# Top-k rounds, masks and evacuations reordered in the mixing stage of a two-block transformer kernel

## The chip, the cores and the metric

The kernel runs on one core of one Trainium2 chip, as one program. Time is device microseconds (us) of one execution. The core's engines are TensorE (PE, its weight loads PEld), VectorE (DVE), ScalarE (ACT), GpSimd (POOL) and SyncE (SP); each runs its own instructions in order, and they wait for each other by semaphores that only count up. Matrix products go into PSUM (8 banks of 128 partitions by 512 float32), everything else lies in SBUF.

## The reference, cut to what matters

Two transformer blocks on 512 tokens of width 1024, all in float32. The change lies in the mixing stage of the second block:

```
z = u @ w_in          # split into aq, ak, av, iq, ik, iw, rq, rk, rv, rg, ga, gb
...
score = sum over 8 index heads of relu(q_idx . k_idx) * w_idx      # per query and key
score = where(admissible, score, -1e30)                            # chunks of 64
top_val, top_pos = top_k(score, 128)
y_a = softmax attention of 8 heads over the selected keys
rq, rk = rope(rq), rope(rk)                     # 4 heads of 128
y_r = group_norm(retention(rq, rk, rv)) * silu(rg)
merged = sigmoid(ga) * (y_a @ w_branch_a) + sigmoid(gb) * (y_r @ w_branch_b)
```

## The kernel before, in words

All products are made in three passes of rounded parts: an operand x is held as a high part and a low part (XH, XL; HH, HL), a weight as WH and WL, and PE adds high*high, low*high and high*low. Weights come in units of 128 x 1024 (512 KB) in one fixed order. SP fetches a unit into one of 4 slots of RAW; POOL rounds it (L326, WH = RAW * 1) and takes the rest (L329, WL = RAW - WH); PE uses it and counts `units_done`, which frees the slot for POOL and SP. Unit n of a feature-major product goes to PSUM bank n mod 4, and DVE counts `evacuated` (started at 4, as are the other unit counts) when a bank has been read. Unit numbers are held in FIRST: the mixing stage has mix_heads from 252, ret_qk from 263, ret_v from 271, ret_gate from 279, merge from 287.

The order around the change, all written out by hand:

- *Index scores.* PE makes the scores of tile t (128 queries against 128(t+1) keys) of 8 heads, ACT takes the relu, DVE adds them up in SC (L1551, L1554). DVE then writes -1e30 where a key may not be seen (L1561) and copies tiles 1 to 3 to MK (L1563). Tile 0 has 128 keys, so all are taken.
- *Top-k.* `take(first, rounds)` does rounds of `max` (the 8 largest of each query, to TOP, L1571) and `match_replace` (those set to -3e38 in MK, L1572). Sixteen rounds give the 128 keys of a tile: rounds 0 to 15 are tile 1 (256 columns), 16 to 31 tile 2 (384), 32 to 47 tile 3 (512).
- *Rotations.* The eight units of ret_qk are rotated by `rotate`: it waits for the unit, does what `between` holds (two rounds of take), waits for ACT's copy with swapped halves (L1077, into bank 7), multiplies by cosine (L1527, which frees the bank), by sine (L1528), adds (L1529).
- *Value halves.* `products_token_major` makes retention's values for 512 of 1024 channels at a time: 4 units, 96 matmuls (L437), into all four banks 0 to 3, one per 128 tokens. PE waits for a bank when it first writes to it, at k = 0. DVE evacuates a half with four instructions (`token_major`, L1448, from PSUM to VT). `order` is the order of the four.
- *Masks.* For each tile DVE makes an additive mask, 0 or -1e30, in MK from SC and MK (L1583 to L1587), from SBUF to SBUF: two `tensor_scalar` for tile 0, three and one `tensor_tensor` for each other tile.
- *Sparse attention.* 16 steps s = 4p + t (head pair p, tile t). PE: scores(s) into banks 4 and 5 (L755), transposes(s-1) (L765), two k steps of the gate products (ret_gate, L371 to L373, banks 2 and 3), values(s-1) into bank 0 or 1 (L776). DVE: adds the mask and takes the maximum (L1608), two reciprocals, one scaling (L1620). ACT: exponentials, the other scaling, copies. scores(s) waits until both heads of s-1 are masked (`a_masked`).

In the kernel before, PE waits ahead of all of this for all four evacuations of the second value half, and the first two gate units wait for them again.

Of the kernel before, what the change touches and what calls it, by code (L numbers as in the profile page):

```python
# [31 lines left out]
TT = SEQ // P  # L32
SLOTS = 4
# [32 lines left out]
FIRST = {name: sum(n for _, n in PRODUCTS[:k]) for k, (name, _) in enumerate(PRODUCTS)}  # L66
# [51 lines left out]
def program(nc, xT, weights, gains, cols, lnb, bs, wsT, rel, pos, ident_d, decay, pT, out):  # L118
    with ExitStack() as ctx:
# [73 lines left out]
        def sem(name):  # L193
            return ctx.enter_context(nc.semaphore(name))
# [6 lines left out]
        evacuated = sem("evacuated")  # L201
# [64 lines left out]
        def n_of(t):  # L266

            return P * (t + 1)

        def off(t):  # L270

            return P * (t * (t + 1) // 2)
# [68 lines left out]
        def _(pe):  # L341
# [28 lines left out]
            def three_passes(bank_, slot, w, xh, xl, k, stop):  # L370
                nc.tensor.matmul(PS[:, bank_, :], WH[:, slot, w], xh[:, k, :], start=(k == 0), stop=False)  # L371
                nc.tensor.matmul(PS[:, bank_, :], WH[:, slot, w], xl[:, k, :], start=False, stop=False)  # L372
                return nc.tensor.matmul(PS[:, bank_, :], WL[:, slot, w], xh[:, k, :], start=False, stop=stop)  # L373

            def together(*units, norm=True):
# [5 lines left out]
                for k in range(tiles):  # L381
                    w = slice(k * P, k * P + P)
                    for s, (_, xh, xl, ready) in enumerate(units):
                        slot = (first + s) % SLOTS
                        if k == 0:
                            pe.wait_ge(weights_split, split.next())
                            pe.wait_ge(evacuated, bank.next())
                            high.next()
                        if ready is xr:
                            if s == 0:  # L390
                                pe.wait_ge(xh_ready, xg.now(back=tiles - 1 - k))
                            if k == tiles - 1 and s >= 2:
                                continue
                            high_passes(slot, w, xh, k)
                    if norm and k == tiles - 1:
                        stat_sum()
                    for s, (_, xh, xl, ready) in enumerate(units):
                        slot = (first + s) % SLOTS
                        if s == 0:
                            pe.wait_ge(ready.sem, ready.now(back=tiles - 1 - k))  # L400
                        if ready is not xr:
                            last = three_passes(slot, slot, w, xh, xl, k, k == tiles - 1)
                        else:
                            if k == tiles - 1 and s >= 2:
                                high_passes(slot, w, xh, k)
                            last = low_pass(slot, w, xl, k, tiles)
                        if k == tiles - 1:
                            last.then_inc(units_done, 1)
                        if norm and k == tiles - 1 and s == 2:
                            stat_spread()  # L410
# [321 lines left out]
            products_token_major()  # L732

            g0 = FIRST["ret_gate"]
            pe.wait_ge(evacuated, g0 + SLOTS)
            pe.wait_ge(rotated, 18)

            def gate_products(first, last):

                for j in range(first, last):  # L740
                    n, k = g0 + j // DT, j % DT
                    if k == 0:
                        pe.wait_ge(weights_split, n + 1 + SLOTS)
                        pe.wait_ge(evacuated, n + 3)
                    end = three_passes(2 + n % 2, n % SLOTS, slice(k * P, k * P + P), XH, XL, k, k == DT - 1)
                    if k == DT - 1:
                        end.then_inc(units_done, 1)
# [21 lines left out]
            def sparse_values(s):  # L769
                p, t = divmod(s, TT)  # L770
                pe.wait_ge(a_turned_out, 2 * s + 2)
                if t == 0 and p >= 2:
                    pe.wait_ge(a_low, p - 1)
                for k in range(t + 1):
                    for hh in range(2):
                        last = nc.tensor.matmul(PS[hh * HD:hh * HD + HD, p % 2, t * P:t * P + P], AVW[:, k, 0:HD],  # L776
                                                PROBT[:, hh, k * P:k * P + P], start=(k == 0), stop=(k == t))
                        if k == t:
                            last.then_inc(a_values, 1)
# [28 lines left out]
            for s in range(steps):  # L808
                sparse_scores(s)
                if s:  # L810
                    sparse_transposes(s - 1)
                gate_products(2 * s, 2 * s + 2)
                if s:
                    sparse_values(s - 1)
            gate_products(32, 34)
            sparse_transposes(steps - 1)
            pe.wait_ge(a_masked, 2 * steps)
            for k in (1, 3, 0):
                ret_scores(0, k)
            sparse_values(steps - 1)  # L820
            ret_scores(0, 2)
            gate_products(34, 38)
            pe.wait_ge(a_low, 4)
            for h in range(4):
# [366 lines left out]
        def _(dve):  # L1191
            dve.sem_inc(evacuated, SLOTS)
            V = nc.vector
            done = Count(units_done, SLOTS)
# [5 lines left out]
            def link(ins):  # L1200

                ins.then_inc(dve_self, 1)
                dve.wait_ge(dve_self, me.next())
# [240 lines left out]
            def token_major(half, order=range(TT)):  # L1444
                first = done.n
                dve.wait_ge(units_done, done.next(4))
                for j in order:
                    V.tensor_scalar(VT[:, j, half * SEQ:half * SEQ + SEQ], PS[:, (first + j) % SLOTS, :],  # L1448
                                    RT[:, 4 + j:5 + j], None, ALU.mult).then_inc(evacuated, 1)
# [27 lines left out]
            for s in range(DT * TT):  # L1477
                p, t = divmod(s, TT)
                n = n_of(t)
# [41 lines left out]
            def rotate(dst, cos, sin, scale, between=None):  # L1521

                src = unit()
                if between:
                    between()
                dve.wait_ge(act_out, ao.next())
                V.scalar_tensor_tensor(T[:, 2, :], src, scale, cos, ALU.mult, ALU.mult).then_inc(evacuated, 1)  # L1527
                link(V.scalar_tensor_tensor(SWAP, SWAP, scale, sin, ALU.mult, ALU.mult))  # L1528
                V.tensor_tensor(dst, T[:, 2, :], SWAP, ALU.add).then_inc(rotated, 1)  # L1529
# [14 lines left out]
            for n in range(32):  # L1544
                t, h = n // 8, n % 8
                s = SC[:, off(t):off(t) + n_of(t)]
# [12 lines left out]
            for t in range(TT):  # L1559
                s = SC[:, off(t):off(t) + n_of(t)]  # L1560
# [4 lines left out]
            def take(first, rounds):  # L1565


                for r in range(first, first + rounds):
                    t = 1 + r // 16
                    work = MK[:, off(t):off(t) + n_of(t)]  # L1570
                    link(V.max(TOP[:], work))  # L1571
                    link(V.match_replace(work, TOP[:], work, TAKEN))  # L1572

            for n in range(8):
                rotate(R1[:, n, :], COS128, SIN128, 1.0 if n % 2 == 0 else P ** -0.5,
                       lambda: take(2 * n, 2))
            for half in range(2):
                take(16 * (half + 1), 16)
                token_major(half)
            for t in range(TT):  # L1580
                c = slice(off(t), off(t) + n_of(t))
                ok = SC[:, c]
                link(V.tensor_scalar(ok, ok, 0.5 * NEG, None, ALU.is_gt))  # L1583
                if t:
                    link(V.tensor_scalar(MK[:, c], MK[:, c], 0.5 * TAKEN, None, ALU.is_lt))
                    link(V.tensor_tensor(ok, ok, MK[:, c], ALU.mult))
                link(V.tensor_scalar(MK[:, c], ok, -NEG, NEG, ALU.mult, ALU.add))  # L1587

            def take_gate(f):

                dve.wait_ge(units_done, FIRST["ret_gate"] + f + 1 + SLOTS)
                V.tensor_tensor(gate_tile(f), PS[:, 2 + (FIRST["ret_gate"] + f) % 2, :], RI[:], ALU.mult)\
                 .then_inc(evacuated, 1)
# [6 lines left out]
            for s in range(4 * TT):  # L1600
                p, t = divmod(s, TT)
                n = n_of(t)
# [249 lines left out]
```

## Time and profile before

| | us |
|---|---|
| median of 3 runs | 2481.31 (2479.49 to 2481.4) |
| the profiled execution | 2479.67 |
| its span in the profile | 2477.9 |
| PE busy | 2399.2 (97%) |
| DVE busy | 1112.5 (45%) |
| ACT busy | 563.3 (23%) |
| POOL busy | 1739.4 (70%) |

Times in the rows further below are microseconds from the span's start. In a timeline a row is: start, duration, engine, line and operation, output<-inputs with partitions x elements, the number of like instructions merged in it (xN), and in brackets the idle time of the engine ahead of it with the engine and instruction that ended it. No bracket means that the engine was idle for next to nothing. An instruction's duration holds what it waits for after it was issued, a busy port for instance.

### The profile page before, as it was taken

The page shows a single profiled execution, that of the slowest core. Times are in us where ns is not written, and L with a number is a line of the kernel's source. Part 1 is how long each engine was busy: PE and PEld are TensorE (multiplying, and loading weights), DVE is VectorE, ACT ScalarE, POOL GpSimd, SP SyncE. Part 2 cuts the span into 40 slices and gives each one's busy share as a digit, 9 for nine tenths or more (in the row PEclk, how much of TensorE's full clock was granted, in tenths as well). Part 3 has the DMA queues.
Part 4 walks back from the last instruction along what each step waited for, and adds up shares of the span by engine and source line. Part 5 has one row for each costly group of instructions (what it writes and reads, how often), then busy time and mean ns, then how long its engine had stood idle before and what let it go on. Part 6 is the DMA issues. An engine that isn't in the chain of part 4 may idle for free.

```text
span 2477.9 us, 31448 instructions
## 1 busy us (share of the span) xinstructions
PE 2399.2 (97%) x11070; PEld 1941.6 (78%) x11070; DVE 1112.5 (45%) x1584; ACT 563.3 (23%) x1039; POOL 1739.4 (70%) x827
## 2 busy tenths in 40 slices
PE   8999999999999999999999999998999999999998
PEld 6777888877777788887888888676678888888876
DVE  3445323454444532447424335478573334342345
ACT  2322101132553210113201013321621121010031
POOL 8657877776445787785888887565248887888765
PEclk9999999999999999999999999999999999999999
DMA  5222333323222233332233323232112333333322
GB/s 180 85 68 85 102 93 100 95 85 100 84 68 69 77 102 95 94 104 77 86 109 93 100 85 100 64 102 68 31 51 89 102 102 94 94 96 99 89 73 77
DMA packets 64665, 221.08 MB, mean 89 GB/s; under 512 B 7360, under 2 KB 9664, under 8 KB 64448
## 3 DMA queue, kind: packets, MB, share of 16 engines
q1 hardware_dynamic: 60336, 210.27, 28.4%
q10 hardware_dynamic: 4240, 9.57, 1.3%
q8 instruction: 62, 1.02, 0.2%
q14 instruction: 27, 0.22, 0.0%
HBM read 217.71 MB, written 2.10 MB: 89 GB/s over the span
## 4 chain that ended last, share of the span: by engine, by line
PE 89%; DVE 6%; ACT 2%; issue 2%; DMA 0%; DVEq 0%; POOL 0%; ACTq 0%; SPq 0%; POOLq 0%
PE PS L366 21%; PE PS L360 21%; PE PS L361 21%; PE PS L437 4%; PE PS L371 4%; PE PS L373 4%; PE PS L372 4%; PE PS L413 1%; PE PS L414 1%; PE PS L417 1%; PE PS L637 1%; DVE MK L1572 1%; PE PS L658 1%; PE PS L647 1%; DVE TOP L1571 1%
## 5 line engine op out<-in xcount | busy, mean ns | idle before, releaser
L326 POOL TENSOR_TENSOR WH<-RAW,ONES 128x1024 fp32r<-128x1024 f32 (+3 forms) x411 | 767.1, 1866 | 682.0 <-PE PS L366 270.8
L329 POOL TENSOR_TENSOR WL<-RAW,WH 128x1024 fp32r<-128x1024 f32 (+3 forms) x411 | 976.8, 2377 | 32.2
L360 PE MATMUL PS<-XH,WH 128*128 128x512 f32 x1568 | 615.9, 393 | 9.8 <-DVE PTL L1698 5.4
L361 PE MATMUL PS<-XL,WH 128*128 128x512 f32 x1568 | 613.2, 391 | 0.0
L366 PE MATMUL PS<-XH,WL 128*128 128x512 f32 x1568 | 387.9, 389 | 0.0
L360 PEld LDWEIGHTS PS<-XH,WH 128*128 128x128 f32 x1568 | 296.4, 189 | 80.1 <-issue 10.9
L361 PEld LDWEIGHTS PS<-XL,WH 128*128 128x128 f32 x1568 | 296.3, 189 | 61.0
L366 PEld LDWEIGHTS PS<-XH,WL 128*128 128x128 f32 x1568 | 294.0, 188 | 62.8 <-issue 1.6
L1312 DVE TENSOR_TENSOR HL<-T,HH 128x512 f32 x108 | 233.5, 2162 | 152.1 <-ACT HH L945 107.7
L360 PE MATMUL PS<-HH,WH 128*128 128x512 f32 x712 | 277.2, 389 | 2.0 <-DVE HL L1632 2.0
L361 PE MATMUL PS<-HL,WH 128*128 128x512 f32 x712 | 277.0, 389 | 0.0
L1342 DVE TENSOR_TENSOR M<-PS,M 128x512 f32 x80 | 55.2, 692 | 312.8 <-PE PS L366 278.1
L366 PE MATMUL PS<-HH,WL 128*128 128x512 f32 x712 | 177.1, 390 | 0.0
L360 PEld LDWEIGHTS PS<-HH,WH 128*128 128x128 f32 x712 | 133.6, 188 | 30.5 <-DVE HL L1632 2.7
L366 PEld LDWEIGHTS PS<-HH,WL 128*128 128x128 f32 x712 | 134.0, 188 | 27.9
L361 PEld LDWEIGHTS PS<-HL,WH 128*128 128x128 f32 x712 | 133.6, 188 | 27.7
L942 ACT ACTIVATE T<-T 128x512 f32<-128x512 f32 x64 | 40.6, 635 | 485.0 <-DVE T L1319 485.0
L1329 DVE TENSOR_TENSOR T<-PS,RI 128x512 f32<-128x512 f32 x44 | 30.4, 691 | 193.1 <-PE PS L366 193.1
L371 PE MATMUL PS<-HH,WH 128*128 128x512 f32 x280 | 110.7, 395 | 5.7 <-POOL WL L329 5.4
L373 PE MATMUL PS<-HH,WL 128*128 128x512 f32 x280 | 109.2, 390 | 0.0
L372 PE MATMUL PS<-HL,WH 128*128 128x512 f32 x280 | 109.0, 389 | 0.0
L957 ACT ACTIVATE HH<-T 128x512 f32 x44 | 27.9, 634 | 279.8 <-DVE T L1332 279.8
(232 smaller groups left out, 2941.4 us busy)
## 6 DMA issues: line engine op xcount, KB each, us to landing
RAW<-in_weights SPq DMA_DIRECT2D x379, 512.0 KB, 3.5
RAW<-in_weights SPq DMA_DIRECT2D x16, 384.0 KB, 3.1
H<-in_xT SPq DMA_DIRECT2D x8, 256.0 KB, 6.4
BIAS<-in_rel ACTq DMA_DIRECT2D x8, 256.0 KB, 3.4
RAW<-in_weights SPq DMA_DIRECT2D x8, 256.0 KB, 2.7
out<-R ACTq DMA_DIRECT2D x8, 256.0 KB, 2.2
BIAS<-in_rel ACTq DMA_DIRECT2D x8, 224.0 KB, 3.8
DECAY<-in_decay ACTq DMA_DIRECT2D x1, 1024.0 KB, 4.7
```

Source lines behind the costliest of these rows:

```text
L326: nc.gpsimd.tensor_tensor(WH[:, slot, 0:w], raw, ONES[:, 0:1].to_broadcast([P, w]), ALU.mult).then_inc(high_split, 1)
L329: nc.gpsimd.tensor_tensor(WL[:, slot, 0:w], raw, WH[:, slot, 0:w].bitcast(F32), ALU.subtract).then_inc(weights_split, 1)
L360: nc.tensor.matmul(PS[:, slot, :], WH[:, slot, w], xh[:, k, :], start=(k == 0), stop=False)
L361: nc.tensor.matmul(PS[:, slot, :], WH[:, slot, w], xl[:, k, :], start=False, stop=False)
L366: last = nc.tensor.matmul(PS[:, slot, :], WL[:, slot, k * P:k * P + P], xh[:, k, :], start=False, stop=(k == tiles - 1))
L371: nc.tensor.matmul(PS[:, bank_, :], WH[:, slot, w], xh[:, k, :], start=(k == 0), stop=False)
L372: nc.tensor.matmul(PS[:, bank_, :], WH[:, slot, w], xl[:, k, :], start=False, stop=False)
L373: return nc.tensor.matmul(PS[:, bank_, :], WL[:, slot, w], xh[:, k, :], start=False, stop=stop)
L437: return nc.tensor.matmul(PS[:, (first + j) % SLOTS, :], x[:, k, j * P:j * P + P], wt[:, slot, kk * SEQ:kk * SEQ + SEQ], start=(k == 0 and ...
L942: S.activation(T[:, 1, :], T[:, 0, :], ACT.Square).then_inc(act_self, 1)
L1312: V.tensor_tensor(HL[:, f, :], T[:, src:src + 1, :], HH[:, f, :].bitcast(F32), ALU.subtract).then_inc(h_ready, 1)
L1342: V.tensor_tensor(M[:, f, :], PS[:, slot:slot + 1, :], M[:, f, :], ALU.add)\
```

## The change

- DVE does three rounds beside each rotation instead of two (24 instead of 16), then 8 rounds.
- The masks of tiles 0 to 2 are made after these, then come 4 rounds of tile 3, then the evacuation of the first value half, then the other 12 rounds.
- The second value half is evacuated with the two gate banks (3 and 2) first, then 0 and 1; the mask of tile 3 follows.
- PE no longer waits for the four evacuations ahead of the attention: the first gate unit waits for one of them, the second for two, and values(0), the first to write to bank 0, for all four.

```diff
             g0 = FIRST["ret_gate"]
-            pe.wait_ge(evacuated, g0 + SLOTS)
             pe.wait_ge(rotated, 18)
...
                     if k == 0:
                         pe.wait_ge(weights_split, n + 1 + SLOTS)
-                        pe.wait_ge(evacuated, n + 3)
+                        pe.wait_ge(evacuated, n + 3 if n >= g0 + 2 else n + 1)
...
             def sparse_values(s):
                 p, t = divmod(s, TT)
                 pe.wait_ge(a_turned_out, 2 * s + 2)
+                if s == 0:
+                    pe.wait_ge(evacuated, g0 + SLOTS)
...
             for n in range(8):
                 rotate(R1[:, n, :], COS128, SIN128, 1.0 if n % 2 == 0 else P ** -0.5,
-                       lambda: take(2 * n, 2))
-            for half in range(2):
-                take(16 * (half + 1), 16)
-                token_major(half)
-            for t in range(TT):
+                       lambda: take(3 * n, 3))
+            def mask(t):
+
                 c = slice(off(t), off(t) + n_of(t))
                 ok = SC[:, c]
                 link(V.tensor_scalar(ok, ok, 0.5 * NEG, None, ALU.is_gt))
...
                 link(V.tensor_scalar(MK[:, c], ok, -NEG, NEG, ALU.mult, ALU.add))
+            take(24, 8)
+            for t in range(3):
+                mask(t)
+            take(32, 4)
+            token_major(0)
+            take(36, 12)
+            g0 = FIRST["ret_gate"]
+            banks = (2 + g0 % 2, 2 + (g0 + 1) % 2, 0, 1)
+            token_major(1, [(b - done.n) % SLOTS for b in banks])
+            mask(3)
```

## Rows read from the trace of the kernel before

**Rows 1.** The page, part 1: busy us (share of the span) xinstructions.

```profile
PE 2399.2 (97%) x11070; PEld 1941.6 (78%) x11070; DVE 1112.5 (45%) x1584; ACT 563.3 (23%) x1039; POOL 1739.4 (70%) x827
```

**Rows 2.** Timeline of PE: start, us, what, [idle before it <-releaser].

```profile
1666.49 0.50 PE L437 MATMUL PS<-WH,XH 128*128 128x512 f32 x1 [0.71 <-DVE T L1527]
...
1688.50 0.50 PE L437 MATMUL PS<-WH,XH 128*128 128x512 f32 x1 [2.00 <-DVE VT L1448]
...
1717.40 0.80 PE L755 MATMUL PS<-AK,AQIQ 64*128 64x128 f32 x4 [6.79 <-DVE VT L1448]
...
1723.68 0.70 PE L755 MATMUL PS<-AK,AQIQ 64*128 64x256 f32 x4 [2.62 <-DVE NMX L1608]
```

**Rows 3.** Timeline of DVE, rotations of ret_qk and the rounds behind.

```profile
1627.95 0.43 DVE L1571 MAX8 TOP<-MK 128x8 f32<-128x256 f32 x1
...
1629.92 0.69 DVE L1527 SCALAR_TENSOR_TENSOR T<-PS,ROT 128x512 f32<-128x512 f32 x1
...
1658.34 0.43 DVE L1571 MAX8 TOP<-MK 128x8 f32<-128x256 f32 x1 [1.45 <-PE PS L366]
...
1665.74 0.69 DVE L1527 SCALAR_TENSOR_TENSOR T<-PS,ROT 128x512 f32<-128x512 f32 x1
...
1667.68 0.56 DVE L1571 MAX8 TOP<-MK 128x8 f32<-128x384 f32 x1
```

**Rows 4.** Timeline of DVE, evacuations, last rounds, masks, first step of the attention.

```profile
1687.69 2.73 DVE L1448 TENSOR_SCALAR VT<-PS,RT 128x512 f32<-128x512 f32 x4
1690.34 0.68 DVE L1571 MAX8 TOP<-MK 128x8 f32<-128x512 f32 x1
...
1714.62 2.73 DVE L1448 TENSOR_SCALAR VT<-PS,RT 128x512 f32<-128x512 f32 x4
1717.26 0.22 DVE L1583 TENSOR_SCALAR SC<-SC 128x128 f32<-128x128 f32 x1
...
1721.00 0.43 DVE L1583 TENSOR_SCALAR SC<-SC 128x512 f32<-128x512 f32 x1
...
1723.11 0.29 DVE L1608 CUSTOM_DVE_ANT_0 PROB<-PS,MK 128x128 f32<-128x128 f32 x1
```

**Rows 5.** Timeline of POOL, the splits of weight units.

```profile
1675.71 1.90 POOL L326 TENSOR_TENSOR WH<-RAW,ONES 128x1024 fp32r<-128x1024 f32 x1 [1.05 <-PE PS L437]
1677.68 2.40 POOL L329 TENSOR_TENSOR WL<-RAW,WH 128x1024 fp32r<-128x1024 f32 x1
1681.15 1.90 POOL L326 TENSOR_TENSOR WH<-RAW,ONES 128x1024 fp32r<-128x1024 f32 x1 [1.06 <-PE PS L437]
...
1712.66 2.35 POOL L329 TENSOR_TENSOR WL<-RAW,WH 128x1024 fp32r<-128x1024 f32 x1
1735.25 1.90 POOL L326 TENSOR_TENSOR WH<-RAW,ONES 128x1024 fp32r<-128x1024 f32 x1 [20.24 <-PE PS L373]
...
1849.93 2.69 POOL L329 TENSOR_TENSOR WL<-RAW,WH 128x1024 fp32r<-128x1024 f32 x1
```

**Rows 6.** Timeline of DVE, two instructions that meet POOL at work.

```profile
1735.99 1.43 DVE L1620 TENSOR_SCALAR PROB<-PROB,RECX 128x512 f32<-128x512 f32 x1
...
1850.32 2.84 DVE L1632 SCALAR_TENSOR_TENSOR HL<-R,GAIN,HH 128x512 fp32r<-128x512 f32 x1
```

**Rows 7.** The page, part 5: a group of instructions | busy us, mean ns | idle before.

```profile
L1312 DVE TENSOR_TENSOR HL<-T,HH 128x512 f32 x108 | 233.5, 2162 | 152.1 <-ACT HH L945 107.7
```

**Rows 8.** Windows: us, busy PE, PEld, DVE, ACT, POOL, then PEclk, DMA share, GB/s.

```profile
1689.00:1692.00 3.00, 3.00 (x14) 2.37 (x14) 2.93 (x7) 0.00 (x0) 1.96 (x1) 1.00 0.00 0
...
1714.50:1715.00 0.50, 0.00 (x0) 0.00 (x0) 0.47 (x2) 0.00 (x0) 0.50 (x1) 0.78 0.00 0
...
1717.00:1720.00 3.00, 2.60 (x8) 1.99 (x9) 2.74 (x9) 0.00 (x0) 0.00 (x0) 0.50 0.28 113
...
1721.50:1722.00 0.50, 0.00 (x0) 0.00 (x0) 0.47 (x2) 0.00 (x0) 0.00 (x0) 0.89 0.00 0
1726.00:1729.00 3.00, 3.00 (x13) 1.56 (x11) 0.68 (x3) 1.01 (x5) 0.00 (x0) 0.59 0.00 0
```

## The prediction

> **What bounds the kernel now.** I read the page's busy line first: TensorE (PE) is busy for 97% of the span [rows 1]. So a change matters only where PE stands still, and the mixing stage has the one long place: 6.79 us for VectorE (DVE) at 1710.6 us, then 2.62 us more at 1721 [rows 2]. Next, DVE's timeline: it shows why PE waits. From 1667.68 on DVE has no gap in brackets: sixteen rounds of 384 columns, four evacuations, sixteen rounds of 512 columns, four evacuations, the masks, and at 1723.11 the first L1608 of the sparse attention [rows 3, 4]. DVE is the bound there, though in the rotations before it it stood idle, mostly 1.45 us each time [rows 3]. L1608 is the point of account: PE's second scores follow 0.57 us behind it [rows 2, 4], then PE is nearly gapless, so what L1608 gains or loses the end does too. Last, GpSimd's (POOL) timeline beside DVE's, since the change moves work in time: POOL stands idle for 20.24 us from 1715.0, but at 1679 it works [rows 5, 6].
>
> **The rounds, step by step.** Prices from DVE's starts: a round of 256 columns 0.98 (1627.95 to 1629.92 for two), a rotation 1.94 (1665.74 to 1667.68), a round of 384 (1687.69 - 1667.68) / 16 = 1.25, of 512 (1714.62 - 1690.34) / 16 = 1.52, an evacuation of a half 2.65, masks of tiles 0 to 2 3.74, of tile 3 2.11 [rows 3, 4]. PE delivers a unit each 5.44 us (POOL's WH, one per unit, from 1675.71 to 1681.15, [rows 5]), ret_qk's seventh at 1658.34 [rows 3], so the sixth at 1652.9 and the last at 1663.8. Three rounds and a rotation take 4.88, less than 5.44, so rotations 0 to 4 end at 1652.4 and the idle time there is used up. Rotation 5 (one round of 256, two of 384) ends at 1658.3; rotations 6 and 7 with 3 x 1.25 + 1.94 = 5.69 end at 1664.0 and 1669.7. So DVE is eight rounds ahead at 1669.7, and 2.04 us later than now.
>
> That 2.04 us goes to PE: token-major products need rotation 7's bank, and waited 0.71 us for it, until 1666.49 [rows 2]. Now 2.75 us. The first half ends at 1688.55 instead of 1686.51. DVE needs it only at token_major(0), which comes later, so this costs nothing by itself; it does move POOL 2.04 us later.
>
> Rounds 24 to 31 end DVE's stretch at 1669.7 + 10.0 = 1679.7. Were the masks as cheap as at 1717, they would end at 1683.5, four rounds at 1689.5, and PE would restart 1.84 us later than now, at 1690.34 (now 1688.50, [rows 2]), ending at 1712.45. Then 2.65 + 2.11 give L1608 at 1717.25, a gain of 5.9 us. I don't believe the masks are that cheap.
>
> **The masks beside POOL.** All fourteen mask instructions read and write SBUF alone (eleven `tensor_scalar`, three `tensor_tensor` with two SBUF inputs). At 1717 they ran while POOL was idle: 0.43 us for 512 columns [rows 4, 5]. The same form while POOL worked, L1620 at 1735.99, took 1.43 us and ended at 1737.42, 0.27 after POOL's WH from 1735.25 ended at 1737.15 [rows 5, 6]. The subtraction HL<-T,HH has two SBUF inputs and takes 2162 ns in the mean [rows 7], where L1527 with the same 512 columns and one input in PSUM takes 0.69 us [rows 3]. And DVE cannot slip several through: the second of two such instructions in a row, L1632 at 1850.32, took 2.84 us, until 0.54 after POOL's WL from 1849.93 ended at 1852.62 [rows 5, 6]. So each such DVE instruction that meets POOL at work waits out one POOL instruction (WH 1.90, WL 2.40), then POOL takes its turn. It ends its own time less about 0.15 after POOL's (0.43 - 0.15 = 0.28). Rounds and evacuations do not suffer: their prices are flat across POOL's work [rows 4, 5].
>
> POOL, 2.04 us later: WL from 1679.72 to 1682.12, WH from 1683.19, WL behind it, WH from 1688.63 [rows 5]. The chain of ten instructions (two of tile 0, four of tile 1, four of tile 2):
> first waits until 1682.12, ends 1682.2; second, third and fourth run in POOL's pause to 1683.1; the fifth (0.42) starts 1683.14, 0.05 before WH, ends 1683.56; sixth waits for WH, ends 1685.45; seventh waits for WL, ends 1688.0; eighth and ninth fall in the next pause, to 1689.0; tenth waits for WH, ends 1690.95. That is 7.5 us more than 1683.5. If the fifth loses to WH by a hair, and the ninth too, the end is 1693.4. And if the 2.75 us wait lowers PE's clock (a wait of 2.62 us was followed by such a stretch, [rows 2, 8]; one of 2.00 us at 1686.5 was not, [rows 2, 8]), POOL is up to 1.7 us later still, and the same count gives 1692.5. I take 1691.7.
>
> On the hair's breadth the Trainium skill has a rule ("SBUF — State Buffer", section "Who interferes with whom"): in its words, "Whoever issues first gets the shared pair for the whole instruction". By that rule the fifth wins and the chain ends at 1690.95; the other way it would be 1693.4. No row here shows so close a meeting; the waits of 1.43 and 2.84 us agree with the rule otherwise.
>
> Rounds 32 to 35: 6.1, so token_major(0) at 1697.8 instead of 1687.69, 10.1 later. PE restarts 0.81 behind, at 1698.6, after almost 10 us of standing. After 6.79 us of standing its granted clock was 0.50, and full again at 1721.5, 4.1 us after the restart at 1717.40 [rows 2, 8]; half of 4.1 is lost, 2.1 us (bounds 0 and 3.4, the latter if the low stretch holds for 6.8 us behind the restart, as the whole stretch from 1714.8 to 1721.5 lasted). The second half takes 1710.61 - 1688.50 = 22.1, so it ends at 1698.6 + 22.1 + 2.1 = 1722.8. DVE's 2.65 + 12 x 1.52 would let it be ready at 1718.7: from here PE's end decides, and DVE idles 4 us. Evacuations until 1725.5.
>
> Then mask(3) meets POOL too: POOL starts the freed slot's WH when the half ends and its WL 2.05 us after it, 2.35 long [rows 5], so until 1727.2. The first of four mask instructions ends 0.28 after that, the other three have POOL idle: 1.65. L1608 at 1729.1, against 1723.11: **+6.0 us**.
>
> **The gate edits.** Gate banks first and single waits let PE do scores(0) and its first two gate k steps (six matmuls) while DVE still evacuates; their result is due only when PE has had L1608's word for scores(1). Before, PE was done with them at 1721.1 and stood 2.62 us [rows 2]; after, it stands over 3 us. Off the path: 0 (bounds -0.3 and +0.8, by whether a low clock, as at 1726 [rows 8], covers more or less of the steps behind scores(1)). The wait moved to sparse_values(0) is long fulfilled there (evacuations end 1725.5, it comes after 1730): 0; behind it on PE's queue is only the attention itself. No DMA is moved; SP and POOL are only later with weights, with slots full.
>
> **Sum.** Profiled execution 2479.67 + 6.0 = 2485.7. The median of the runs shown is 2481.31, 1.64 above the profiled one; I forecast the median: 2481.31 + 6.0 = 2487.3 us.
>
> **Rivals.**
> 1. Masks run free beside POOL: the sum without waits, -5.9, 2475.4 us. For it: the rounds, also on SBUF data, are not delayed. Against: L1620, the same form as the masks, is [rows 6]. This is the case on the faster side; it decides by one thing, whether the ten mask instructions take 3.7 us or about 11; below some 5 us of waits in all it would win.
> 2. DVE waits once and then keeps its turn, since mask instructions follow 0.03 us apart. The masks then end at 1682.1 + 3.7 = 1685.9, PE's half at 1715 to 1716, mask(3) waits once: L1608 at 1721.3 to 1722.4, -1.8 to -0.7: about 2480.0 us. Against: L1632's second one [rows 6].
> 3. Waits as forecast, but PE loses no clock behind its stop: +3.9, 2485.2 us. For it only that a stop's recovery varies; against it [rows 8].
> 4. Waits as forecast, with the fifth and ninth lost: +1.7 on the forecast, 2489.0 us.
>
> **How the numbers follow.** Forecast 0.52; rival 3 0.12; rival 4 0.16; rival 1 0.11; rival 2 0.09. The forecast's own range, from the clock's and the alignment's bounds, is 2485 to 2490. Stretched to rival 2's time and beyond rival 4's by the clock's bound: 2480 to 2491.5; rival 1 is left out. The 0.2% that a measurement of this kernel can tell from no change is 5.0 us, so faster is under 2476.3, slower over 2486.3. Slower: rival 4, and some 0.85 of the forecast, 0.60. Faster: rival 1, 0.11. Same: the rest, 0.29.
>
> **What would show it.** Right: in the changed kernel the mask instructions of tiles 0 to 2 span about 11 us and several last 1.5 to 2.5 us, each ending just behind a POOL instruction; rounds stay 0.98, 1.25 and 1.52; PE waits some 10 us for VT before the second half and starts it at a clock of 0.50; DVE idles some 4 us before the second evacuation; rotations show no idle but one of 0.5 us; first L1608 near 1729. Wrong: masks spanning 3.7 us, PE waiting about 1.4 us at that place, and L1608 at 1717; or full clock behind the stop.

## The result and the profile after

The changed kernel takes 2485.37 us (median of 10 runs, 2483.64 to 2489.0), the kernel before, in runs beside them, 2480.53 us (median of 10, 2475.99 to 2486.56). The ratio is 1.0022, 95% interval 1.0013 to 1.003: slower. Of 2480.53 us that is 5.5 us (3.2 to 7.4); the two medians differ by 4.8. The profiled execution took 2485.23 us, and its span is 2483.4 against 2477.9: 5.5 us as well.

Lines have shifted: the rounds are L1572 and L1573, masks L1582 to L1586, value evacuation L1449, the mask added in a step L1617, scores L754. The first round of top-k starts at 1628.58 here and at 1627.95 in the rows of before. That difference arose earlier, where the two programs do the same work: over the ten profiled executions of this document the first round starts anywhere from 1624.37 to 1632.37. So I take as the stage's length the time from there to the first mask added: 1723.11 - 1627.95 = 95.16 before, 1728.20 - 1628.58 = 99.62 after. The stage has 4.46 of the 5.5 us; the other 1.0 lies outside it.

The waits of PE between 1560 and 1870 us in the changed kernel (engine, line, waited for, us in total, times, longest), which answer to [rows 2]:

```profile
PE PS L437 <- DVE VT L1449: 9.1, 1, 9.1
...
PE PS L754 <- DVE NMX L1617: 4.3, 1, 4.3
PE PS L437 <- DVE T L1528: 2.7, 1, 2.7
...
PE PS L371 <- DVE VT L1449: 0.6, 1, 0.6
```

The 6.79 us before the attention is gone. In its place stand 9.14 us before the second value half (2.00 before), 2.74 for rotation 7 (0.71) and 4.30 before the second scores (2.62). DVE's timeline shows what stands in front of the 9.14 (as [rows 4], with its columns):

```profile
1628.58 0.43 DVE L1572 MAX8 TOP<-MK 128x8 f32<-128x256 f32 x1
...
1680.35 0.23 DVE L1582 TENSOR_SCALAR SC<-SC 128x128 f32<-128x128 f32 x1
1680.62 2.30 DVE L1586 TENSOR_SCALAR MK<-SC 128x128 f32<-128x128 f32 x1
1682.95 0.29 DVE L1582 TENSOR_SCALAR SC<-SC 128x256 f32<-128x256 f32 x1
1683.28 0.29 DVE L1584 TENSOR_SCALAR MK<-MK 128x256 f32<-128x256 f32 x1
1683.61 0.42 DVE L1585 TENSOR_TENSOR SC<-SC,MK 128x256 f32<-128x256 f32 x1
1684.07 1.87 DVE L1586 TENSOR_SCALAR MK<-SC 128x256 f32<-128x256 f32 x1
1685.97 2.50 DVE L1582 TENSOR_SCALAR SC<-SC 128x384 f32<-128x384 f32 x1
1688.50 0.36 DVE L1584 TENSOR_SCALAR MK<-MK 128x384 f32<-128x384 f32 x1
1688.89 0.56 DVE L1585 TENSOR_TENSOR SC<-SC,MK 128x384 f32<-128x384 f32 x1
1689.49 1.93 DVE L1586 TENSOR_SCALAR MK<-SC 128x384 f32<-128x384 f32 x1
1691.45 0.69 DVE L1572 MAX8 TOP<-MK 128x8 f32<-128x512 f32 x1
...
1697.52 2.73 DVE L1449 TENSOR_SCALAR VT<-PS,RT 128x512 f32<-128x512 f32 x4
...
1721.93 2.73 DVE L1449 TENSOR_SCALAR VT<-PS,RT 128x512 f32<-128x512 f32 x4 [3.60 <-PE PS L437]
1724.58 1.93 DVE L1582 TENSOR_SCALAR SC<-SC 128x512 f32<-128x512 f32 x1
1726.55 0.43 DVE L1584 TENSOR_SCALAR MK<-MK 128x512 f32<-128x512 f32 x1
...
1728.20 0.29 DVE L1617 CUSTOM_DVE_ANT_0 PROB<-PS,MK 128x128 f32<-128x128 f32 x1
```

Ten instructions from 1680.35 to 1691.45, 11.10 us, where the same ten took 3.74 [rows 4]. Six have the old duration, four last 1.87 to 2.50 us. POOL's timeline tells which:

```profile
1680.36 2.47 POOL L329 TENSOR_TENSOR WL<-RAW,WH 128x1024 fp32r<-128x1024 f32 x1
1683.83 1.96 POOL L326 TENSOR_TENSOR WH<-RAW,ONES 128x1024 fp32r<-128x1024 f32 x1 [1.00 <-PE PS L437]
1685.86 2.39 POOL L329 TENSOR_TENSOR WL<-RAW,WH 128x1024 fp32r<-128x1024 f32 x1
1689.27 1.94 POOL L326 TENSOR_TENSOR WH<-RAW,ONES 128x1024 fp32r<-128x1024 f32 x1 [1.02 <-PE PS L437]
```

POOL's four end at 1682.83, 1685.79, 1688.25 and 1691.21; the four long instructions of DVE end at 1682.92, 1685.94, 1688.47 and 1691.42, each 0.09 to 0.22 behind one. What comes in POOL's pauses (1682.83 to 1683.83, 1688.25 to 1689.27) is short. The mask of tile 3 pays once more, 1.93 us at 1724.58. All five long instructions are `tensor_scalar`; the rounds (MAX8, MATCH_REPLACE8), which also go from SBUF to SBUF, keep their lengths beside the same work of POOL.

The second value half runs partly at the low clock (columns as in [rows 8]; PE restarts at 1698.33):

```profile
1698.00:1701.00 3.00, 2.67 (x6) 2.15 (x7) 2.97 (x7) 0.00 (x0) 0.00 (x0) 0.50 0.01 3
1702.00:1705.00 3.00, 3.00 (x15) 2.49 (x14) 2.86 (x7) 0.00 (x0) 0.00 (x0) 1.00 0.00 0
```

Six matmuls in 3 us, then fifteen. The half takes 1721.93 - 1698.33 = 23.6 us where it took 22.1, and DVE, done with its rounds, waits 3.60 us for it.

### The profile page after: what moved, and what is told of

It is laid out like the page before. It is cut to its first block, busy times and chain, and to the rows that moved or that the text cites. A ratio compares the mean times of both kernels' runs of the same rounds, so it can differ in the third digit from the quotient of the medians.

```text
span 2483.4 us, 31448 instructions
## 1 busy us (share of the span) xinstructions
PE 2400.0 (97%) x11070; PEld 1942.4 (78%) x11070; DVE 1121.0 (45%) x1584; ACT 561.9 (23%) x1039; POOL 1738.7 (70%) x827
## 4 chain that ended last, share of the span: by engine, by line
PE 89%; DVE 5%; POOL 2%; ACT 2%; issue 1%; DMA 0%; DVEq 0%; POOLq 0%; ACTq 0%; SPq 0%
PE PS L366 21%; PE PS L360 21%; PE PS L361 20%; PE PS L437 5%; PE PS L371 4%; PE PS L373 4%; PE PS L372 4%; POOL WL L329 1%; PE PS L413 1%; POOL WH L326 1%; PE PS L414 1%; PE PS L417 1%; PE PS L637 1%; PE PS L658 1%; PE PS L647 1%
## 5 line engine op out<-in xcount | busy, mean ns | idle before, releaser
L437 PE MATMUL PS<-WH,XH 128*128 128x512 f32 x192 | 71.2, 413 | 25.4 <-DVE VT L1449 10.2
```

Source lines behind the costliest of these rows:

```text
L437: return nc.tensor.matmul(PS[:, (first + j) % SLOTS, :], x[:, k, j * P:j * P + P], wt[:, slot, kk * SEQ:kk * SEQ + SEQ], start=(k == 0 and ...
```

## The experiments

Theory A is the prediction's: mask instructions from SBUF to SBUF wait for POOL's running instruction. Theory B: the third round beside the rotations holds up PE through rotation 7, and masks are slow in that place for another reason. Ratios are to the kernel before in runs beside each, with their 95% intervals. The stage's length is always first round to first mask added, both as the profiled execution has them. Behind the first mask added, the ten profiled executions take 754.1 to 755.2 us, but for experiments 7 (752.9) and 8 (751.7).

| | ratio | stage, us | first round at | first mask added at |
|---|---|---|---|---|
| before | 1 | 95.16 | 1627.95 | 1723.11 |
| changed kernel | 1.0022 (1.0013 to 1.003) | 99.62 | 1628.58 | 1728.20 |
| 1 masks through PSUM | 0.9984 (0.9975 to 0.9993) | 91.05 | 1628.04 | 1719.09 |
| 2 masks last | 1.0 (0.9991 to 1.0009) | 93.74 | 1632.37 | 1726.11 |
| 3 before, masks through PSUM | 1.0 (0.9991 to 1.0009) | 95.30 | 1628.78 | 1724.08 |
| 4 before, POOL busy | 1.0031 (1.0019 to 1.0044) | 101.66 | 1626.19 | 1727.85 |
| 5 before, gate edits | 1.0001 (0.9992 to 1.001) | 95.16 | 1624.37 | 1719.53 |
| 6 changed, PE kept busy | 1.0019 (1.001 to 1.0028) | 98.47 | 1627.19 | 1725.66 |
| 7 before, masks moved | 1.0005 (0.9996 to 1.0014) | 98.14 | 1626.46 | 1724.60 |
| 8 masks through PSUM, tile 3's early | 0.9961 (0.9947 to 0.9975) | 88.01 | 1630.18 | 1718.19 |

### 1. The changed kernel with masks through PSUM

```diff
-                ok = SC[:, c]
-                link(V.tensor_scalar(ok, ok, 0.5 * NEG, None, ALU.is_gt))
+                ok = PS[:, 6, 0:n_of(t)]
+                link(V.tensor_scalar(ok, SC[:, c], 0.5 * NEG, None, ALU.is_gt))
                 if t:
-                    link(V.tensor_scalar(MK[:, c], MK[:, c], 0.5 * TAKEN, None, ALU.is_lt))
-                    link(V.tensor_tensor(ok, ok, MK[:, c], ALU.mult))
+                    link(V.scalar_tensor_tensor(ok, MK[:, c], 0.5 * TAKEN, ok, ALU.is_lt, ALU.mult))
```

> The changed kernel, with the intermediate results of the masks in PSUM bank 6 instead of SBUF: three instructions per tile (two for tile 0), none of which reads two SBUF operands or goes from SBUF to SBUF. Theory A (the mask instructions wait for POOL's running instruction): no mask instruction waits; the ten instructions (now eight) of tiles 0 to 2 span about 4 us instead of 11.1, PE stands under 2 us before the second value half instead of 9.1, the first L1608-type instruction (mask added in step 0) comes at 1717.5 to 1718 instead of 1728.2, and the time is about 10 us under the changed kernel's, 5 us under the kernel before. Theory B (three rounds beside each rotation, by delaying rotation 7 and PE behind it, cost the time; the masks would take as long anywhere at that place): the masks stay near 11 us and the time stays at the changed kernel's.

DVE's timeline of this kernel in the same place:

```profile
1679.80 0.29 DVE L1582 TENSOR_SCALAR PS<-SC 128x128 f32<-128x128 f32 x1
...
1681.84 0.56 DVE L1582 TENSOR_SCALAR PS<-SC 128x384 f32<-128x384 f32 x1
1682.43 0.56 DVE L1584 SCALAR_TENSOR_TENSOR PS<-MK,PS 128x384 f32<-128x384 f32 x1
1683.03 0.56 DVE L1585 TENSOR_SCALAR MK<-PS 128x384 f32<-128x384 f32 x1
...
1689.70 2.73 DVE L1449 TENSOR_SCALAR VT<-PS,RT 128x512 f32<-128x512 f32 x4
...
1719.09 0.29 DVE L1616 CUSTOM_DVE_ANT_0 PROB<-PS,MK 128x128 f32<-128x128 f32 x1
```

and POOL's beside it:

```profile
1679.79 2.40 POOL L329 TENSOR_TENSOR WL<-RAW,WH 128x1024 fp32r<-128x1024 f32 x1
1683.26 1.89 POOL L326 TENSOR_TENSOR WH<-RAW,ONES 128x1024 fp32r<-128x1024 f32 x1 [1.06 <-PE PS L437]
```

The masks lie under the same POOL instructions, and none waits: 3.8 us (until the next round at 1683.62) instead of 11.1, and POOL's instructions are 2.40 and 1.89 long, not 2.47 and 1.96. The stage loses 8.6 us, time falls from 1.0022 to 0.9984 of before: 3.8 us under the kernel before where 5 were expected. The first mask is added at 1719.09, later than the 1717.5 to 1718 expected: the granted clock was 0.50 from 1691.1 to 1694.5, behind a stop of 1.89 us, and the second half took 23.77 us instead of 22.1. PE's 2.74 us wait for rotation 7 is here as in the changed kernel, so theory B has no part in the loss.

### 2. The changed kernel with all masks last

```diff
             take(24, 8)
-            for t in range(3):
-                mask(t)
             take(32, 4)
...
-            mask(3)
+            for t in range(TT):
+                mask(t)
```

> The changed kernel with all four masks behind the second evacuation, where the kernel before has them. Theory A: of fourteen mask instructions only the first waits for POOL (its last WL of the half, about 1.5 us); the first value half is evacuated at about 1688.6, PE stands 1.7 us there; step 0 of the attention at about 1721.6 against 1723.1 of the kernel before: 1.5 us faster than before, 6 us faster than the changed kernel. Theory B: PE's delay by rotation 7 (2 us) goes through to the end, so about 2 us slower than before.

```profile
1718.75 1.74 DVE L1582 TENSOR_SCALAR SC<-SC 128x128 f32<-128x128 f32 x1
```

One mask instruction waits; the stage is 1.42 us shorter than before, as expected. In time that is 0.06%, inside this comparison's interval, so the time alone says only that the loss is gone: three rounds and gate edits without the moved masks are no slower.

### 3. The kernel before with masks through PSUM

The edit of experiment 1 on the kernel before.

> Control: the kernel before with masks through PSUM bank 6, at their old place, where POOL is idle. Theory A: the form alone gives nothing, since nobody is waited for: masks 5.9 us as before, time within 0.5 us of the kernel before. Theory B': the form by itself (eleven instead of fourteen instructions) is what is faster: 2 us or more.

95.30 against 95.16, the masks 5.99 us instead of 5.85: the form by itself is worth nothing where POOL is idle.

### 4. The kernel before with POOL kept at work

```diff
                         pool.wait_ge(high_split, high.next())
+                        if u + s == FIRST["ret_gate"] + 3:
+                            for again in range(4):
+                                nc.gpsimd.tensor_tensor(WL[:, slot, 0:w], raw, WH[:, slot, 0:w].bitcast(F32),
+                                                        ALU.subtract).then_inc(pool_go, 1)
+                                pool.wait_ge(pool_go, again + 1)
```

The list of units, which SP and POOL alone read, is split beside it, so that this unit stands outside a loop.

> The kernel before, in which POOL computes WL of the fourth gate unit five times over (same values), so that it is at work from 1712.7 until about 1725 us, while DVE makes the masks; no other instruction is changed. Theory A: about four of the fourteen mask instructions wait out one POOL instruction of 2.4 us each, the masks span about 12 us instead of 5.85, and the time grows by 6 to 7 us. Theory B: POOL's work off the critical path changes nothing: masks 5.85 us, time within 0.5 us.

POOL's and DVE's timelines:

```profile
1710.93 9.64 POOL L331 TENSOR_TENSOR WL<-RAW,WH 128x1024 fp32r<-128x1024 f32 x4
1720.66 2.34 POOL L334 TENSOR_TENSOR WL<-RAW,WH 128x1024 fp32r<-128x1024 f32 x1
```

```profile
1715.51 0.28 DVE L1588 TENSOR_SCALAR SC<-SC 128x128 f32<-128x128 f32 x1
1715.82 2.40 DVE L1592 TENSOR_SCALAR MK<-SC 128x128 f32<-128x128 f32 x1
1718.26 2.47 DVE L1588 TENSOR_SCALAR SC<-SC 128x256 f32<-128x256 f32 x1
1720.76 2.38 DVE L1590 TENSOR_SCALAR MK<-MK 128x256 f32<-128x256 f32 x1
1723.18 0.42 DVE L1591 TENSOR_TENSOR SC<-SC,MK 128x256 f32<-128x256 f32 x1
```

Nothing of DVE or PE is touched, and the masks take 1727.85 - 1715.51 = 12.3 us instead of 5.85; one DVE instruction gets through per POOL instruction, and when POOL ends at 1723.0 the rest is as fast as ever. Three waited out a whole POOL instruction where about four were expected; the `tensor_tensor` came after POOL's end. The stage grows by 6.5 us, the time by 0.31% (7.3 us between medians). This is the cause added by itself.

### 5. The gate edits alone

```diff
-            pe.wait_ge(evacuated, g0 + SLOTS)
...
-                        pe.wait_ge(evacuated, n + 3)
+                        pe.wait_ge(evacuated, n + 3 if n >= g0 + 2 else n + 1)
...
+                if s == 0:
+                    pe.wait_ge(evacuated, g0 + SLOTS)
...
+            token_major(1, [(b - done.n) % SLOTS for b in banks])
```

> The gate edits alone on the kernel before: banks 3 and 2 evacuated first, gate units waiting for one and two evacuations, the wait for all four ahead of values(0). Expected: PE begins scores(0) at once after the second half (1710.6 instead of 1717.4) and its first gate steps 2 us earlier than before, then stands until the masks are done; L1608 of step 0 stays at 1723.1; time within 0.5 us of the kernel before. A rival: the earlier, separate work keeps the clock up and gives 1 to 2 us.

```profile
1711.93 0.77 PE L371 MATMUL PS<-XH,WH 128*128 128x512 f32 x1 [4.49 <-DVE VT L1449]
...
1720.09 1.22 PE L754 MATMUL PS<-AK,AQIQ 64*128 64x256 f32 x4 [5.26 <-DVE NMX L1612]
```

PE's stop is only divided in another way: 4.49 and 5.26 us instead of 6.79 and 2.62. Stage 95.16, to the hundredth that of before. The clock isn't kept up either: the granted clock was 0.50 from 1711.3 to 1724.9 us.

### 6. The changed kernel with PE kept busy in its stop

```diff
-            products_token_major()
+            token_major_half()
+            for k in range(32):
+                nc.tensor.matmul(PS[:, 6, :], XH[:, k % DT, 0:P], XH[:, k % DT, :], start=True, stop=True)
+            token_major_half()
```

> The changed kernel with 32 matmuls without use (XH by XH into bank 6, 7.3 us in all) between the two value halves, where PE stood 9.1 us. Expected: PE starts the second half when it did, at full clock instead of 0.50; the 1.5 us that the low clock cost the second half come back, and time is 1.5 us under the changed kernel's. If the clock cost nothing there, no difference.

```profile
1697.00:1700.00 3.00, 2.78 (x12) 2.32 (x13) 2.96 (x7) 0.00 (x0) 0.00 (x0) 1.00 0.00 0
```

Twelve matmuls in this window instead of six. The half takes 1719.39 - 1697.22 = 22.17 us: 1.43 less than in the changed kernel. The stage is 1.15 shorter. The two times (1.0019 and 1.0022) can't be told apart; the 1.4 us rests on the traces.

This trace also holds the two close meetings that the count of the prediction turned on:

```profile
1678.95 2.40 POOL L329 TENSOR_TENSOR WL<-RAW,WH 128x1024 fp32r<-128x1024 f32 x1
1682.42 2.15 POOL L326 TENSOR_TENSOR WH<-RAW,ONES 128x1024 fp32r<-128x1024 f32 x1 [1.06 <-PE PS L437]
```

```profile
1678.96 2.48 DVE L1585 TENSOR_SCALAR SC<-SC 128x128 f32<-128x128 f32 x1
...
1682.39 0.42 DVE L1588 TENSOR_TENSOR SC<-SC,MK 128x256 f32<-128x256 f32 x1
```

Here the first mask instruction starts 0.01 us behind WL and waits it out, as forecast. The fifth starts 0.03 us ahead of WH, keeps its 0.42 us, and WH takes 2.15 us instead of 1.89.

### 7. The masks of tiles 0 to 2 moved, alone

```diff
             take(16, 16)
+            for t in range(3):
+                mask(t)
             token_major(0)
             take(32, 16)
             token_major(1)
-            for t in range(TT):
-                mask(t)
+            mask(3)
```

> The kernel before with one edit: the masks of tiles 0 to 2 between the sixteen rounds of tile 2 and the evacuation of the first value half; rotations keep two rounds, PE its waits. Theory A: two of the ten mask instructions wait (for WH until 1688.5 and WL until 1691.0), then POOL is out of units and the rest is free: the ten span 6.5 us, the evacuation begins at 1694.2, step 0 of the attention at about 1725.9: 2.8 us slower than before. Without the waits it would be 0.

```profile
1686.21 0.87 DVE L1580 TENSOR_SCALAR SC<-SC 128x128 f32<-128x128 f32 x1
1687.11 2.38 DVE L1584 TENSOR_SCALAR MK<-SC 128x128 f32<-128x128 f32 x1
```

The stage is 2.98 us longer, with these two long instructions and then eight free ones, since PE's stop leaves POOL without units. In time 1.0005, its interval holds both 0 and the 2.8 expected: inconclusive by itself, and in line by the trace. What the stage lost, this execution had back outside it: 1.5 us ahead of the stage and 1.9 us behind it.

### 8. Masks through PSUM, tile 3's ahead of the evacuation

To experiment 1 is added:

```diff
-            token_major(1, [(b - done.n) % SLOTS for b in banks])
             mask(3)
+            token_major(1, [(b - done.n) % SLOTS for b in banks])
```

> The changed kernel with masks through PSUM and tile 3's mask ahead of the second evacuation, in the time in which DVE waits for PE's second half. Expected: another 2 us under the first experiment (masks through PSUM alone), 12 us under the changed kernel and 7 to 8 us under the kernel before, if mask instructions are free of waits there while POOL works (theory A with PSUM as the way out). If the waits come back, no gain over the first experiment.

```profile
1713.36 0.69 DVE L1582 TENSOR_SCALAR PS<-SC 128x512 f32<-128x512 f32 x1
1714.09 0.69 DVE L1584 SCALAR_TENSOR_TENSOR PS<-MK,PS 128x512 f32<-128x512 f32 x1
1714.82 0.69 DVE L1585 TENSOR_SCALAR MK<-PS 128x512 f32<-128x512 f32 x1
1715.55 2.73 DVE L1449 TENSOR_SCALAR VT<-PS,RT 128x512 f32<-128x512 f32 x4
1718.19 0.28 DVE L1616 CUSTOM_DVE_ANT_0 PROB<-PS,MK 128x128 f32<-128x128 f32 x1
```

2470.25 us against 2478.86: ratio 0.9961 (0.9947 to 0.9975), the fastest version, clear of both kernels. Stage 88.01, 7.15 under before and 11.6 under the changed kernel. Under experiment 1 it is 3.04 where 2 were expected: 2.2 for the mask of tile 3, and 0.9 because the second evacuation no longer waits for a half of PE that the low clock had made longer.

The 8.6 us between the medians are more than the stage's 7.15. In the profiled pair another 3.1 us come from behind the stage (751.7 against 754.8). There the granted clock was 1.00 from 1718 to 1900 in this kernel, while the kernel before had stretches of 3.4 us at 0.50 from 1725.0 and from 1854.7. Whether that follows from the edit was not tested.

Here the idea behind the reordering pays, once its masks are out of POOL's way.

## Why the prediction was right

All times below are the changed kernel's less 0.63, the difference of the first round's start.

- *Rounds and rotations.* Rotation 7 made PE wait 2.74 us (2.75 forecast). PE's first half ended at 1698.33 - 9.14 - 0.63 = 1688.56 (1688.55). Rounds of 384 and 512 columns kept 1.25 and 1.52.
- *The masks beside POOL.* The count of the ten gave 1690.95, measured 1690.79. Even the places are nearly the same: the sixth, seventh and tenth wait, as counted; only the first slipped in 0.01 us before WL, and the second waited instead (in experiment 6 it is the first, as counted). The fifth and the ninth, 0.22 and 0.38 ahead of WH, won, so rival 4 did not happen. I had then raised 1690.95 to 1691.7, for the case that one of them lost or that PE's clock fell behind the 2.75 us wait. Neither came in this execution: PE's granted clock was 1.00 throughout the first half. That addition was wrong here, and it carries through as 0.9.
- *PE's loss by the clock.* Forecast 2.1, measured 23.60 - 22.11 = 1.5, and experiment 6, where the half took 22.17, gives 1.43 back. The clock was full again 3.1 us after the restart and not 4.1. This is the second term that was mis-sized.
- *PE's end decides, then mask(3).* The second evacuation at 1721.30 (1722.8 forecast: 0.9 for the masks and 0.6 for the clock), DVE idle 3.60 (4), the first mask of tile 3 at 0.28 behind POOL's end, as computed.
- *The gate edits* at 0: in experiment 5 the stage is the same to the hundredth. PE's stop before the second scores, forecast at over 3 us, was 4.30.
- *Sum.* First mask added at 1727.57 instead of the forecast 1729.1: +4.46, not +6.0. To this come 0.63 from ahead of the stage and 0.4 from behind it in this pair of executions, which make the 5.5 of the profiles; the prediction had no term for them, and that they bring the profiles closer to its 6.0 is luck. Between medians it was 4.8. The forecast 2487.3 was 1.9 us too high; it stood on a median of 2481.31 for the kernel before, which in ten runs was 2480.53. That base carries 0.8 of the 1.9, the effect 1.1. By the line that the prediction drew for slower (over 2486.3, from the same base) 2485.37 is not slower; that it is slower rests on the ratio's interval, which leaves out 1.

The measured median is nearest to the number of rival 3 (2485.2, no clock lost behind the stop), yet that rival is wrong: the clock was at 0.50 and cost 1.4 to 1.5 us. The total is low for other reasons, 0.9 on the masks, 0.6 on the clock's size and 0.8 on the base, against 0.4 from outside the stage.

Rival 1 (masks run free) is what experiment 1 makes of the kernel: -4.1 us in the stage and a ratio of 0.9984, its -5.9 less the 1.7 us of a low clock stretch. Rival 2 (DVE keeps its turn) falls with the four long instructions of the changed kernel and with experiment 4: one DVE instruction gets in between two of POOL's, and no second.

## What to carry to other kernels

Before an instruction of VectorE is moved in time, look at what GpSimd does at the new place: here a `tensor_scalar` from SBUF to SBUF that cost 0.2 to 0.4 us beside an idle GpSimd cost 1.9 to 2.5 us beside a busy one, and a chain of small ones paid again and again. It isn't every instruction from SBUF to SBUF: the rounds of `max` and `match_replace` kept their lengths. So look in the trace for the very form that is to be moved. Of two ways out, a quiet stretch of GpSimd or intermediate results in PSUM, the second kept the freedom to place the work (experiments 1 and 8), at 0.56 us per instruction of 384 columns instead of 0.36. And an order that fills an idle stretch must be counted with the lengths that the work will have there, not with those from where it stood.

## What the runs showed of the hardware that had not been expected

Two instructions of VectorE and GpSimd met within 0.01 us, once in each order. In the changed kernel the mask instruction came first (L1582 at 1680.35, WL at 1680.36): it went through in 0.23 us, and WL was 2.47 us long instead of 2.40 (why not longer, when the mask's 0.23 us reach 0.22 beyond WL's start, no run here tells). In experiment 6 WL came first (1678.95, the mask at 1678.96): WL kept its 2.40, and the mask took 2.48. The Trainium skill ("SBUF — State Buffer", section "Who interferes with whom") says that the first of the two to issue holds the shared ports for its whole instruction. As to who goes first, both traces agree with it down to that hundredth. When POOL's instruction ends, a waiting instruction of VectorE gets its turn ahead of POOL's next one, and only one does (three in a row took 2.40, 2.47 and 2.38 us in experiment 4): that is what made the chain pay four times.

A stop of 2.74 us of PE lowered its clock in one execution and not in others of nearly the same program: behind it the granted clock was 0.50 from 1672.2 to 1675.6 in experiment 8, and 1.00 throughout the first half in the changed kernel and in experiments 1, 2 and 6. Behind a shorter stop, the 1.89 us before the second half of experiment 1, it was 0.50 for 3.4 us; behind the 2.00 us at that place in the kernel before it stayed at 1.00.
